# A two-block fp32 layer stack on one Trainium2 core: five of the second block's first twelve projection chunks as split products, their low parts made by adding transfers

## The chip, the cores and the metric

The kernel runs on one core of one Trainium2 chip. The metric is the device time of one execution in microseconds. The kernel before was timed three times: median 1872.24 us, lowest 1869.12, highest 1878.97.

## What is computed

The input x is 256 tokens by 1024 features, fp32. Two blocks follow each other, each with two layers. The first block has in each layer a mixer of three branches (a state space branch, a latent attention, a gated recurrence), a cross attention to 256 memory rows and a feed-forward part of width 2816. The second block, where the change is, does in each layer:

```python
h = rmsnorm_2(x, g_attn[l])
proj = jnp.einsum('bsd,dc->bsc', h, w_in[l])          # 1024 -> 2304
qa, ka, va, qb, kb, vb = jnp.split(proj, offs, axis=-1)
...
x = x + jnp.einsum('bsm,md->bsd', y, w_out[l])
h = rmsnorm_2(x, g_ffn[l])
gate, val = jnp.split(jnp.einsum('bsd,df->bsf', h, w_up[l]), 2, axis=-1)
gate = centred_dwconv(gate, conv_w[l], conv_b[l])
x = x + jnp.einsum('bsf,fd->bsd', jax.nn.silu(gate) * val, w_down[l])
```

## The kernel before, in words

All activations stay on the chip; the weights stream through once. A weight chunk is 128 partitions by up to 1024 fp32 values (512 KB). SyncE loads the chunks in the order in which TensorE's program names them into a ring of four slots (W, RSLOTS, line 1254); chunk n may be loaded when chunk n-4 is released (chunk_release).

There are two ways to multiply. **Whole**: TensorE takes the fp32 chunk from W as it is (product, line 400; the trace has two rows for one such matmul). **Split, in halves**: every operand is a high part, rounded to fp32r, and a low part, the rest; three products, high x high, high x low and low x high, go to the same bank (line 402). A split chunk has a high part in WH and a low part in WL, each a ring of three slots (HSLOTS). The list splits says who makes the low part: "dve" and "pool" mean that ScalarE copies W to WH (split_to of ScalarE, line 1465) and DVE or POOL then subtracts (low_parts, line 1178); "both" means that POOL does both (both_parts, lines 1349 and 1351). The release of a whole chunk is TensorE's last matmul on it, that of a split chunk the making of its low part. In the first block's gate projections every other chunk of 256 rows by 512 columns is "both" and the ones between are whole; their input has its halves made by POOL (halves_of, lines 1368 and 1369) in mix_half, which lies in the tile HTL.

**Around the change.** Each feed-forward part ends with four banks of 128 tokens by 512 columns, finished in the order of bank_order (last_two). DVE adds each bank to X (add_bank, line 2117). TensorE transposes X into banks "hT" 0 to 3, two groups of 128 features each (raw_T, line 492): hT 0 and 1 ahead of the last bank's products, hT 2 and 3 after the first chunk of the next projection, since they need the last sums. ScalarE evicts hT 0 and 2 (whole_cols of ScalarE, the copies of line 1465 into M), DVE hT 1 and 3 (whole_cols of DVE, lines 2104 and 2105); the input of the projections, HT2, lies in M. Between these ScalarE takes the sums of squares (sum_of, line 1505), from which POOL makes the root of the norm (norm_rstd, lines 1306 to 1317). The root is applied at the eviction of the projections, so TensorE doesn't wait for it.

In the first layer of the second block there is the first block's final norm too: DVE scales X (line 2636), ScalarE takes its squares again (line 1929), and POOL makes the mask of the attention window (lines 1428 to 1431), which ScalarE copies to fp32r.

The second block's projections are p2 0 to p2 4 (proj, token_steps): p2 0 to 3 of 512 columns in four chunks of 256 input rows (k0 = 0, 2, 4, 6), p2 4 of 256 columns in two chunks. All are whole. p2 0, 1 and 2 are TensorE's first work of the layer, with the transposes of the first results (qk_T) between them; p2 3 and 4 are spread between the attention's heads. ScalarE evicts each bank twice, squares (line 1945) and values (take_proj, line 1566); DVE then norms and rotates the heads (norm_rope, lines 2663 to 2694), and TensorE transposes these.

## Time and profile before

| | |
|---|---|
| three runs, median | 1872.24 us (1869.12 to 1878.97) |
| profiled execution, its own time | 1873.33 us |
| its span in the trace | 1871.5 us |
| mean granted TensorE clock | 0.99 |
| TensorE matmuls busy | 95% |
| VectorE (DVE) busy | 66% |
| ScalarE (ACT) busy | 47% |
| GpSimd (POOL) busy | 14% |
| bytes read from HBM | 271.78 MB |

The page lists busy time by engine, the chain of work that ended last, and groups of instructions by line and tile. Times in the trace are microseconds from the span's start. PE is TensorE's matmuls, PEld its weight loads, SPq and POOLq the queues that issue DMAs. A row such as "W,M" names what is read: for a matmul the moving operand first, the stationary one second. "issue" is time in which the engine waited for nothing that the profile shows. A clock of 1.00 is 2.4 GHz, 0.50 is 1.2 GHz.

### The profile page before, as it was taken

How to read it: one execution, taken by the hardware profiler on the slowest of the kernel's cores; microseconds unless marked ns; L12 is line 12 of the kernel's file. 1: busy time of each engine (PE TensorE's matmuls, PEld its weight loads, DVE VectorE, ACT ScalarE, POOL GpSimd, SP SyncE). 2: the span in 40 equal slices, each digit the busy share in tenths (PEclk: the TensorE clock that was granted, in tenths of full speed). 3: DMA queues.
4: the chain of work that ended last, by engine and by line, in shares of the span. 5: the costliest groups of instructions: out<-in, count | busy, mean ns of one | idle time of the engine just before them, and what ended most of it. 6: DMA issues, size and time to landing. Idle time of an engine off the chain costs nothing.

```text
span 1871.5 us, 27092 instructions
## 1 busy us (share of the span) xinstructions
PE 1786.2 (95%) x10038; PEld 1437.7 (77%) x10038; DVE 1236.3 (66%) x1903; ACT 872.1 (47%) x1421; POOL 255.6 (14%) x262
## 2 busy tenths in 40 slices
PE   7999999989999999999989999998999999899998
PEld 6676667679998856668578998656899874679987
DVE  7996746555667893756556566565677746566775
ACT  4224455464344422445455445446555543555553
POOL 4015553010000002455111000100100000010000
PEclk9999999999999999999999999999999999999999
DMA  6445442445556444444254666431455644235664
GB/s 162 135 131 157 135 158 91 156 127 171 160 183 190 114 131 130 158 135 158 78 170 144 186 184 192 142 119 57 135 173 181 196 149 124 68 113 171 181 189 136
DMA packets 192359, 274.61 MB, mean 147 GB/s; under 512 B 25616, under 2 KB 129540, under 8 KB 192228
## 3 DMA queue, kind: packets, MB, share of 16 engines
q1 hardware_dynamic: 191364, 269.86, 47.1%
q0 software_dynamic: 864, 3.02, 0.5%
q8 instruction: 80, 1.31, 0.3%
q14 instruction: 51, 0.42, 0.1%
HBM read 271.78 MB, written 1.05 MB: 146 GB/s over the span
## 4 chain that ended last, share of the span: by engine, by line
PE 86%; DVE 6%; ACT 3%; issue 2%; SPq 1%; DMA 0%; POOL 0%; DVEq 0%; ACTq 0%; POOLq 0%
PE bank L402 52%; PE bank L400 24%; DVE WL L1178 2%; PE bank L676 2%; PE bank L590 1%; PE bank L1034 1%; ACT WH L1465 1%; PE bank L598 1%; PE bank L877 1%; PE bank L492 1%; PE bank L1054 1%; ACT HTH L1465 1%; DVE HTL L2179 1%; PE bank L647 0%; PE bank L659 0%
## 5 line engine op out<-in xcount | busy, mean ns | idle before, releaser
L1178 DVE TENSOR_TENSOR WL<-W,WH 128x1024 fp32r<-128x1024 f32 x312 | 382.3, 1225 | 251.5 <-ACT WH L1465 243.1
L1465 ACT ACTIVATE WH<-W 128x1024 fp32r<-128x1024 f32 x332 | 351.8, 1060 | 273.9 <-PE bank L402 241.3
L402 PE MATMUL bank<-HTH,WH 128*128 128x256 f32 x1536 | 439.7, 286 | 13.2 <-issue 5.2
L402 PE MATMUL bank<-HTL,WH 128*128 128x256 f32 x1536 | 435.9, 284 | 0.0
L402 PE MATMUL bank<-HTH,WL 128*128 128x256 f32 x1536 | 435.9, 284 | 0.0
L402 PEld LDWEIGHTS bank<-HTH,WH 128*128 128x128 f32 x1536 | 296.0, 193 | 18.1 <-issue 11.6
L402 PEld LDWEIGHTS bank<-HTL,WH 128*128 128x128 f32 x1536 | 296.0, 193 | 0.2
L402 PEld LDWEIGHTS bank<-HTH,WL 128*128 128x128 f32 x1536 | 296.0, 193 | 0.0
L402 PE MATMUL bank<-WH,HTL 128*128 128x512 f32 x672 | 262.0, 407 | 0.0
L402 PE MATMUL bank<-WH,HTH 128*128 128x512 f32 x480 | 193.6, 403 | 17.6 <-ACT M L1594 11.4
L402 PE MATMUL bank<-WL,HTH 128*128 128x512 f32 x480 | 188.9, 394 | 0.0
L400 PE MATMUL bank<-W,M 128*128 128x512 f32 (+1 forms) x416 | 166.2, 555 | 2.6 <-issue 2.6
L402 PEld LDWEIGHTS bank<-WH,HTL 128*128 128x128 f32 x672 | 127.3, 189 | 32.3 <-issue 5.3
L400 PE MATMUL bank<-W,HTF 128*128 128x512 f32 (+1 forms) x384 | 149.8, 539 | 0.0
L400 PEld LDWEIGHTS bank<-W,M 128*128 128x128 f32 x416 | 79.2, 194 | 75.7 <-issue 72.9
L402 PEld LDWEIGHTS bank<-WH,HTH 128*128 128x128 f32 x480 | 91.1, 190 | 42.0 <-issue 16.3
L400 PEld LDWEIGHTS bank<-W,HTF 128*128 128x128 f32 x384 | 68.2, 190 | 67.5 <-issue 66.1
L1306 POOL TENSOR_SCALAR QSQ<-QSQ 128x2 f32<-128x2 f32 x9 | 5.5, 608 | 762.3 <-ACT PB L1505 762.3
L402 PEld LDWEIGHTS bank<-WL,HTH 128*128 128x128 f32 x480 | 91.3, 190 | 18.2
L400 PE MATMUL bank<-HTF,W 128*128 128x256 f32 x448 | 99.6, 381 | 0.6 <-DVE HTF L2428 0.6
L400 PEld LDWEIGHTS bank<-HTF,W 128*128 128x128 f32 x448 | 84.3, 190 | 13.2 <-issue 1.1
L1351 POOL TENSOR_TENSOR WL<-W,WH 128x1024 fp32r<-128x1024 f32 x36 | 88.9, 2469 | 2.9
(405 smaller groups left out, 2445.6 us busy)
## 6 DMA issues: line engine op xcount, KB each, us to landing
W<-in_w_in SPq DMA_DIRECT2D x132, 512.0 KB, 3.7
W<-in_ffn_w_gate_up SPq DMA_DIRECT2D x176, 256.0 KB, 3.3
W<-in_w_up SPq DMA_DIRECT2D x176, 256.0 KB, 3.5
W<-in_ffn_w_down SPq DMA_DIRECT2D x44, 512.0 KB, 4.3
W<-in_w_down SPq DMA_DIRECT2D x44, 512.0 KB, 4.3
W<-in_w_out SPq DMA_DIRECT2D x32, 512.0 KB, 3.3
W<-in_ssm_w_glu SPq DMA_DIRECT2D x16, 512.0 KB, 4.3
W<-in_x_w_kv SPq DMA_DIRECT2D x16, 512.0 KB, 3.9
```

The lines of the kernel that those rows point to most:

```text
L400: return pe.matmul(out, at_a(a), at_b(b), start=start, stop=stop, skip_group_check=True)
L402: m = pe.matmul(out, at_a(a[x]), at_b(b[y]), start=(start and i == 0), stop=(stop and i == 2), skip_group_check=True)
L492: m = pe.transpose(ps[:, k * S + tt * P:k * S + tt * P + P], X[:, tt, (2 * j + k) * P:(2 * j + k) * P + P], IDENT[:, :])
L590: ins = pe.matmul(ps[:, tt * S:tt * S + S], qT[:, tt * P:tt * P + P], kT, start=(tt == 0), stop=(tt == TT - 1), skip_group_check=True)
L598: ins = pe.transpose(ps[:, kt * S + tt * P:kt * S + tt * P + P], p_buf(tag, m[1])[:, tt, kt * P:kt * P + P], IDENT[:, :])
L676: m = pe.matmul(ps[:, h * P:h * P + P], ka[:, h, b * P:b * P + P], qa[:, h, b * P:b * P + P], start=(h == 0), stop=(h == HGH - 1), skip_gr ...
L877: m = pe.matmul(ps[64 * (h % 2):64 * (h % 2) + 64, 0:S], vtok[:, kt, h * VD:h * VD + VD], PT[h % 2][:, kt, :], start=(kt == 0), stop=(kt = ...
L1034: pe.matmul(ps[:, tt * S:tt * S + S], qkT[r:r + 64, h // 2, tt * P:tt * P + P], qkT[r:r + 64, 4 + h // 4, :], start=(tt == 0), stop=False, ...
L1054: m = pe.matmul(ps[:, h * HD:h * HD + HD], t_buf("a2", h)[:, kt, tt * P:tt * P + P], proj2[:, kt, 640 + (h // 4) * HD:640 + (h // 4) * HD ...
L1178: eng.tensor_tensor(WL[:, m % HSLOTS, 0:width], W[:, n % RSLOTS, 0:width], h, ALU.subtract)\
L1351: signal(pool.tensor_tensor(low, raw, high.bitcast(F32), ALU.subtract), s, v)
L1465: copy = lambda dst, src, scale=1.0: act.activation(dst, src, ACT.Copy, scale=scale)
```

## The change

Of the twelve chunks of p2 0, 1 and 2 in each layer of the second block, five become split: k0 = 6 of p2 0, k0 = 2 and 6 of p2 1 and of p2 2. The split kind is new, "dma": ScalarE writes the negative of the rounded chunk into WL, then the high part into WH, and POOL issues a DMA that adds the chunk from HBM once more onto WL (add_chunk, accum_op), which leaves the low part. The slot in W is released when ScalarE has made the high part. The two chunks of a pair are named, and so loaded, the split one first; TensorE uses them in the old order (in_pairs).

The split input is made by POOL from HT2 with halves_of into mix_half: first k = 2, 3, then k = 6, 7. TensorE waits for both (in2_halves) after the transposes that follow p2 0's first chunk. In the second block's first layer POOL's root of the final norm goes behind this work, and the mask of the window, which stood behind the root, goes ahead of it. ScalarE makes the first chunk's copies after its third sum of squares and ahead of the eviction of hT 2, the second chunk's after the fourth sum, the third's ahead of the evictions of p2 0, the last two chunks' ahead of those of p2 1.

```diff
--- before.py
+++ after.py
@@ -319,14 +319,24 @@
-            who = "dve" if splits[m][1] == "dve" else "pool"
-            return f"low_{who}", sum(1 for _, w in splits[:m + 1] if (w == "dve") == (who == "dve"))
+            who = splits[m][1]
+            if who == "dma":
+                return f"low_dma{m % HSLOTS}", 16 * sum(1 for _, w in splits[m % HSLOTS:m + 1:HSLOTS] if w == "dma")
+            if who == "dve":
+                return "low_dve", sum(1 for _, w in splits[:m + 1] if w == "dve")
+            return "low_pool", sum(1 for _, w in splits[:m + 1] if w in ("pool", "both"))
...
+        def negative_done(m):
+            return sum(1 for _, w in splits[:m + 1] if w == "dma")
@@ -358,21 +368,45 @@
-            def chunk(name, srcs, k, cols, low="dve"):
+            def declare(name, srcs, k, cols, low="dve"):
...
                 chunks.append((name, srcs, k, cols))
-                if low is None:
+                if low is not None:
+                    m = split_of[n] = len(splits)
+                    splits.append((n, low))
+                    chunk_release[n] = ("high", high_done(m)) if low == "dma" else low_done(m)
+                return n
+            def operands(n):
+                _, _, k, cols = chunks[n]
+                shaped = lambda t, i: t[:, i, 0:k * cols].rearrange("p (k n) -> p k n", k=k)
+                if n not in split_of:
                     pe.wait_ge(sem[f"w_full{n % RSLOTS}"], raw_full(n))
-                    return n, W[:, n % RSLOTS, 0:k * cols].rearrange("p (k n) -> p k n", k=k)
-                m = len(splits)
-                splits.append((n, low))
-                split_of[n] = m
+                    return shaped(W, n % RSLOTS)
+                m = split_of[n]
+                if splits[m][1] == "dma":
+                    pe.wait_ge(sem["high"], high_done(m))
                 s, v = low_done(m)
                 pe.wait_ge(sem[s], v)
-                chunk_release[n] = (s, v)
-                return n, [w[:, m % HSLOTS, 0:k * cols].rearrange("p (k n) -> p k n", k=k) for w in (WH, WL)]
+                return [shaped(w, m % HSLOTS) for w in (WH, WL)]
+            def chunk(*args):
+                n = declare(*args)
+                return n, operands(n)
+            def in_pairs(tag, wname, l, K, c0, cols, kstep, added):
+                n = {}
+                for k0 in range(0, K, 2 * kstep):
+                    for k in (k0 + kstep, k0) if k0 + kstep in added else (k0, k0 + kstep):
+                        n[k] = declare(tag, rows(wname, l, k, kstep, c0, cols), kstep, cols, "dma" if k in added else None)
+                    yield n[k0]
+                    yield n[k0 + kstep]
@@ -407,12 +441,19 @@
-            def token_steps(tag, wname, l, act, K, c0, cols, low="dve", kstep=2, halves=None):
+            def token_steps(tag, wname, l, act, K, c0, cols, low="dve", kstep=2, halves=None, added=()):
                 ps = [begin(*tag, tt) for tt in range(TT)]
+                if added:
+                    numbers = in_pairs(tag, wname, l, K, c0, cols, kstep, added)
                 for k0 in range(0, K, kstep):
                     src, slot = act, lambda k: k
-                    if halves and k0 // kstep % 2:
+                    if added:
+                        n = next(numbers)
+                        if k0 in added:
+                            src, slot = halves, half_slot
+                        w = operands(n)
+                    elif halves and k0 // kstep % 2:
                         n, w = chunk(tag, rows(wname, l, k0, kstep, c0, cols), kstep, cols, "both")
@@ -1024,7 +1065,8 @@
                     return token_steps(("p2", l, j), "w_in_2", l, HT2, KT, 512 * j, 512 if j < 4 else 256, low=None,
-                                       kstep=kstep)
+                                       kstep=kstep, halves=mix_half if j < 3 else None,
+                                       added=(() if j > 2 else (2, 6) if j else (6,)))
@@ -1095,6 +1137,7 @@
                             raw_T(nrm - 1, i, ("f2d", l - 1) if l else ("ffd", DEPTH - 1))
+                        pe.wait_ge(sem["in2_halves"], 2 * l + 2)
                     for _ in steps:
@@ -1350,11 +1393,23 @@
+            def add_chunk(m):
+                n, _ = splits[m]
+                _, (src,), k, cols = chunks[n]
+                pool.wait_ge(sem["negative"], negative_done(m))
+                dst = WL[:, m % HSLOTS, 0:k * cols].rearrange("p (k n) -> p k n", k=k)
+                pool.dma_start(dst, src, accum_op=ALU.add).then_inc(sem[low_done(m)[0]], 16)
...
                         both_parts(m)
+                        lows[0] = m + 1
+                    elif splits[m][1] == "dma":
+                        add_chunk(m)
                         lows[0] = m + 1
@@ -1422,17 +1477,29 @@
                 .then_inc(sem["final_gain"], 16)
-            norm_rstd(nrm)
-            nrm += 1
...
+                first = split_before["p2", l, 0, TT - 1] - 1
+                wait_full(pool, (*(("f2d", l - 1) if l else ("ffd", DEPTH - 1)), *bank_order[-1]))
+                wait_freed(pool, ("hT", nrm + (l == 0), 1))
+                signal(halves_of(mix_half, HT2, 2), "in2_halves", 2 * l + 1)
+                split_to(first + 1)
+                wait_freed(pool, ("hT", nrm + (l == 0), 3))
+                signal(halves_of(mix_half, HT2, 6), "in2_halves", 2 * l + 2)
+                if l == 0:
+                    norm_rstd(nrm)
+                    nrm += 1
+                split_to(first + 2)
                 norm_rstd(nrm, halves=l > 0)
                 nrm += 1
+                split_to(first + 5)
                 for g in range(DFH):
@@ -1483,6 +1550,8 @@
                         act.wait_ge(sem[s], v)
+                    if who == "dma":
+                        signal(copy(WL[:, m % HSLOTS, 0:width], W[:, n % RSLOTS, 0:width], -1.0), "negative", negative_done(m))
                     signal(copy(WH[:, m % HSLOTS, 0:width], W[:, n % RSLOTS, 0:width]), "high", high_done(m))
@@ -1906,8 +1975,10 @@
             sum_of(nrm, ("ffd", DEPTH - 1), 0, 1, 2)
+            split_to(split_before["p2", 0, 0, TT - 1])
             whole_cols(nrm + 1, HT2, final_gain, 2)
             sum_of(nrm, ("ffd", DEPTH - 1), 3)
+            split_to(split_before["p2", 0, 0, TT - 1] + 1)
             nrm += 1
@@ -1920,8 +1991,10 @@
                     sum_of(nrm, ("f2d", l - 1), 0, 1, 2)
+                    split_to(split_before["p2", l, 0, TT - 1])
                     whole_cols(nrm, HT2, own_gain, 2)
                     sum_of(nrm, ("f2d", l - 1), 3)
+                    split_to(split_before["p2", l, 0, TT - 1] + 1)
                 else:
@@ -1934,6 +2007,9 @@
+                    if j < 2:
+                        split_to(split_before["p2", l, 0, TT - 1] + 2 * j + 2)
                     for tt in range(TT):
```

## Rows read from the trace of the kernel before

**Rows 1.** The page: busy time by engine; shares of the chain that ended last.
```profile
PE 1786.2 (95%) x10038; PEld 1437.7 (77%) x10038; DVE 1236.3 (66%) x1903; ACT 872.1 (47%) x1421; POOL 255.6 (14%) x262
...
PE 86%; DVE 6%; ACT 3%; issue 2%; SPq 1%; DMA 0%; POOL 0%; DVEq 0%; ACTq 0%; POOLq 0%
```

**Rows 2.** The chain in the gate stage, layer 1: start us, us, what.
```profile
747.90 2.73 PE bank L402 x12
750.64 3.43 PE bank L400 x8
```

**Rows 3.** TensorE's timeline, second block: start us, us, engine, line, operation, tiles, count.
```profile
1195.87 1.04 PE L492 MATMUL bank<-IDENT,X 128*128 128x128 f32 x8
1196.74 24.20 PE L400 MATMUL bank<-W,M 128*128 128x512 f32 x56
...
1221.65 13.90 PE L400 MATMUL bank<-W,M 128*128 128x512 f32 x32
1235.39 0.60 PE L1022 MATMUL bank<-IDENT,M 128*128 128x128 f32 x4
...
1532.83 24.20 PE L400 MATMUL bank<-W,M 128*128 128x512 f32 x56
```

**Rows 4.** The timeline of ScalarE, DVE and POOL beside it, both layers.
```profile
1193.66 0.19 ACT L1505 ACTIVATION_READ_ACCUMULATOR PB<-X 128x1 f32 x1
1196.51 0.98 ACT L1465 ACTIVATE M<-bank,PAR 128x256 f32<-128x256 f32 x2 [2.66 <-PE bank L492]
...
1198.06 0.19 ACT L1505 ACTIVATION_READ_ACCUMULATOR PB<-X 128x1 f32 x1
...
1197.54 0.48 DVE L2105 TENSOR_SCALAR M<-bank,PAR 128x256 f32<-128x256 f32 x1
...
1198.39 0.19 POOL L1309 TENSOR_TENSOR SSQ<-QSQ 128x2 f32<-128x2 f32 x1 [4.85 <-ACT PB L1505]
...
1533.63 0.48 DVE L2105 TENSOR_SCALAR M<-bank,PAR 128x256 f32<-128x256 f32 x1
1534.15 2.25 DVE L2653 TENSOR_TENSOR TB<-RC,BT 128x64 f32<-128x64 f32 x16
```

**Rows 5.** POOL's instructions on the tile HTL: durations in ns, forms.
```profile
L1368 POOL CAST HTL<-HTF x4: 609/610/758, 135.9 to 728.8; 128x512 fp32r<-128x512 f32 x4
L1369 POOL TENSOR_TENSOR HTL<-HTF,HTL x4: 1263/1268/2126, 136.7 to 729.5; 128x512 fp32r<-128x512 f32 x4
```

**Rows 6.** The page's costliest groups: ScalarE's copies of a chunk.
```profile
L1465 ACT ACTIVATE WH<-W 128x1024 fp32r<-128x1024 f32 x332 | 351.8, 1060 | 273.9 <-PE bank L402 241.3
```

**Rows 7.** The timeline of ScalarE and DVE later in the projections, layer 0.
```profile
1208.02 0.69 ACT L1945 ACTIVATE TB<-bank,RSTD 128x512 f32<-128x512 f32 x1 [2.06 <-issue]
...
1219.32 0.69 ACT L1945 ACTIVATE TB<-bank,RSTD 128x512 f32<-128x512 f32 x1 [8.46 <-PE bank L400]
...
1232.32 0.42 DVE L2688 TENSOR_TENSOR A<-A,TB 128x256 f32<-128x256 f32 x1
```

**Rows 8.** DMA issues: KB each, median us from issue to landing.
```profile
W<-in_w_in SPq DMA_DIRECT2D x132, 512.0 KB, 3.7
...
M<-in_norm_final POOLq DMA_DIRECT2D x1, 512.0 KB, 7.5
```

**Rows 9.** Stretches (busy us by engine, granted clock, DMA) and TensorE's timeline there.
```profile
488.00:490.00 2.00, 0.00 (x0) 0.01 (x1) 1.83 (x6) 0.00 (x0) 0.00 (x0) 1.00 0.76 221
490.00:493.40 3.40, 3.37 (x16) 3.40 (x17) 2.09 (x5) 1.85 (x4) 0.00 (x0) 0.50 0.17 60
1295.60:1302.40 6.80, 5.57 (x14) 4.44 (x15) 3.90 (x8) 4.16 (x13) 0.00 (x0) 0.50 0.03 7
1358.00:1366.00 8.00, 6.31 (x53) 6.14 (x52) 6.09 (x10) 4.37 (x7) 0.00 (x0) 1.00 0.52 171
...
1296.84 0.77 PE L402 MATMUL bank<-WH,HTH 128*128 128x512 f32 x1 [5.72 <-ACT M L1594]
...
1361.68 0.35 PE L402 MATMUL bank<-HTH,WH 128*128 128x256 f32 x1 [1.69 <-issue]
```

## The prediction

> **What bounds the kernel now.** The page comes first: TensorE is busy for 95% of the span and is 86% of the chain that ended last [rows 1]. So a microsecond taken from TensorE's products is a microsecond of the kernel, unless the products then wait. Next come the chain in the gate stage, which already alternates whole and halved chunks of this very size, and TensorE's timeline around the changed stage. A chunk of 256 input rows by 512 columns costs 3.43 us whole (eight rows of L400) and 2.73 us in halves (twelve rows of L402) [rows 2]. In the second block's layer 0 the projections run without a gap: a first chunk, the transposes of the input's second half at 1195.87, then seven chunks from 1196.74, two transposes, four chunks from 1221.65, end at 1235.39 [rows 3]. Layer 1 has the same pattern at 1532.83. Here nothing but TensorE is late.
>
> **What the change takes away.** Five chunks of twelve per layer go from 3.43 to 2.73 us: 5 x 0.70 = 3.5 us per layer, **7.0 us in both**, 0.37% of the time. A measurement of this kernel can tell about 0.5%, 9.4 us, from no change; so the full gain would not be seen.
>
> **The new wait on TensorE.** The split input (mix_half) has to be made by POOL, and TensorE waits for all of it (in2_halves at 2l+2) straight after the transposes, ahead of the second chunk, though only the fourth chunk of that projection uses it. Behind this wait stand the second, whole chunk and all else on TensorE. Its cost in layer 0: DVE ends the eviction of k = 6, 7 at 1197.54 + 0.48 = 1198.02; POOL starts some 0.14 us after another engine's signal (its sum at 1198.39 after ACT's read that ends at 1198.25) [rows 4]; POOL makes a half in a cast of 0.61 and a subtraction of 1.27 us, with 0.1 us between, 2.0 us [rows 5]. So the halves are there at 1200.1, TensorE goes on at about 1200.3 in place of 1196.74, and **3.5 us** are lost. The other half (k = 2, 3) is hidden: its input is out before the first chunk starts, and POOL has the length of that chunk and of the transposes for it. In layer 1 the eviction ends at 1534.11, 0.1 us later against its transposes, and DVE then runs sixteen small products with two SBUF inputs, 2.25 us long, beside POOL's subtraction [rows 4]. Rows 5 show that subtraction at 1.26 to 2.13 us. I take 0.4 us more for layer 1; bounds 0 and 0.9. The two stalls make **7.4 us**.
> The Trainium skill (SBUF — State Buffer, Who interferes with whom) says that a DVE instruction with two SBUF inputs holds off a GpSimd instruction that reads SBUF; by that, layer 1 would be at the upper bound. The longest subtraction of rows 5 fits it, but the trace does not show that it is the cause.
>
> **The clock.** After 5.72 us without a matmul the rows show TensorE at half its rate: the granted clock is 0.50 of 2.4 GHz, that is 1.2 GHz, for 6.8 us, of which 1.2 still fell into the idle time. After 2.0 us it was 0.50 for 3.4 us. After 1.69 us it stayed at 1.00 [rows 9]. An idle time of 3.5 us lies between the two that cost. 3.4 us at half speed lose 1.7 us, 6.8 us less 1.2 lose 2.8 us. I take 1.7 per layer, the row that 3.5 is nearest to: **3.4 us**, bounds 0 and 5.6.
>
> **What ScalarE gets.** Ten copies of 1.06 us per layer (minus the weights, then their high part) [rows 6], 10.6 us. Cover in layer 0: the first two start after the third sum, at 1193.9, and end by 1196.0, before the eviction that starts at 1196.51 [rows 4]. The second two wait for a load into the slot that TensorE frees at 1195.87; with the 3.7 us of rows 8 they run from 1199.6 to 1201.8. Evictions began at 1208.02 [rows 7]; the third pair goes ahead of them, so they begin at 1210.2, where the first projection now ends at 1209.9. The last four lie in the 8.46 us in which ScalarE waited for the second projection [rows 7]; they end at about 1219.5 (the last load follows a chunk that TensorE ends at 1213.3), that projection's first bank at 1220.8. If this cover were gone, each pair would put 2.1 us on the evictions. DVE's norm and rotation of the second projection ended at 1232.74, 2.65 us before TensorE wanted them at 1235.39 [rows 3, 7]; it starts about 1.3 us later, so 1.4 us stay. Cost: nothing; bounds 0 and 2 us per layer.
>
> **POOL and the queues.** In layer 0 POOL's root for the final norm goes behind the halves, 2 us later. It feeds the evictions through DVE and ScalarE; even 1.9 us later these would meet the first projection's new end. In layer 1 the root waits for a load and a copy, until about 1539.5, while the first projection ends at about 1546. On SP the loads keep their count, but an added chunk stands ahead of its partner and its slot is free once ScalarE has copied it. The whole chunk behind it is issued when TensorE ends the second chunk, 1203.7, lands at 1207.4 and is wanted at 1209.9: hidden by 2.5 us. The band mask is made earlier. Nothing.
>
> **The adding transfers.** No row shows one. From the end of the negative copy (POOL free) to TensorE's use, layer 0 gives: 1195.0 to 1207.2, 1201.4 to 1213.3, 1209.1 to 1219.5, 1214.1 to 1226.5, 1218.4 to 1232.7; the shortest is **10.4 us**. The nearest rows: 512 KB from SP's queue land in 3.7 us, 512 KB from POOL's in 7.5 us [rows 8]. The lower bound is 3.7; for the upper I double 7.5, since an add has more to do than a load: 15. I take 7.5, the same queue and size: cost 0.
> The Trainium skill (DMA: Bandwidth & Descriptors, Anatomy of one DMA — SWDGE (gpsimd) path) gives a plain transfer on this path 2.0 us plus its bytes by 436 GB/s; an estimate from that page is 3.2 us for 512 KB, and the cost is 0 by it too. The row measured more than twice that.
>
> **The sum.** -7.0 + 7.4 + 3.4 = **+3.8 us**. The profiled execution was 1873.33 us, 1871.5 its span; it goes to 1877.1. The median of the three runs, 1872.24, is 1.1 us below it, so I predict **1876.0 us**.
>
> **The rivals.**
> A, the adds are late: slower. An add stands between ScalarE's copy and the chunk; it decides from 10.4 us on. At 15 us the first is late by 2.8, the second by 0.3, the third by 1.8, the fourth by 0.5 (each lateness lengthens the next one's time): 5.4 per layer, 11 in both, 1887 with the rest. For: accumulating is untried here, and four of five budgets are under 12.5. Against: 7.5 us in the row. Chance 0.13.
> B, the wait without the clock: an idle time of 3.5 us leaves it at 1.00. Then 1872.6. Against: 2.0 us was enough once. For: 1.69 was not. Chance 0.16.
> C, POOL at its slowest, 0.9 us more in each layer, and the clock down for 6.8 us both times: +1.4 and +2.2 on the forecast, 1880; with a copy pair exposed, 1882. Chance 0.12.
> D, TensorE does not stall: the wait is met early and the 7.0 us stay, 1865 to 1869. It would need POOL to be done by 1196.74, before DVE has even evicted its input. Chance 0.04.
> That halving does nothing at all is excluded by rows 2, if these chunks run like the gates'.
> The forecast itself: 0.55.
>
> **How the numbers follow.** Slower by over 0.5% (above 1881.6): nearly all of A, 0.12, half of C, 0.06, and 0.04 of the forecast's case by the unknown copies: 0.22. Faster by over 0.5% (below 1862.9): no case reaches it; 0.02 for what I overlook. Within: 0.76. The range goes from 1868, the upper part of D, to 1886, most of A. B and the forecast lie within it.
>
> **What would show it.** After the transposes of the first projection TensorE idles some 3.5 us, released by POOL's subtraction into HTL, in both layers. The granted clock is 0.50 for 3.4 us or more behind it. Halved chunks show as 2.73 us at full clock, and the projections of layer 0 then end some 2 us later than at 1235.39 against the end of the block before. POOL's add lands within 10 us and no L402 matmul waits on WL. ScalarE's evictions of the second projection start when its bank is full. It is wrong if TensorE waits for a DMA, if no idle time stands behind the transposes, or if the clock stays at 1.00.

## The result, and the profile after

The kernel after took **1886.37 us** (median of six runs, 1883.77 to 1893.46); the kernel before, timed beside it, 1874.46 us (six runs, 1869.12 to 1885.58). The ratio is **1.0066, 95% interval 1.0041 to 1.0090**: the medians are 11.9 us apart and the ratio makes it 12.4 us slower, where 3.8 were forecast. 1886.37 lies 0.4 us above the range of the prediction, and "the same within 0.5%" was given 0.76. Of the 10.4 us between it and the forecast of 1876.0, 2.2 are the kernel before itself, whose median was 1872.24 us when the forecast was made. The profiled execution took 1884.42 us, its span 1882.5, 11.0 more than before.

The page first, the rows that answer to [rows 1]: TensorE's busy time fell by 4.7 us while the span grew by 11.0, so the time is in waits. The chain has more DVE (6 to 8%) and 1% of DMA.

```profile
PE 1781.5 (95%) x10078; PEld 1444.7 (77%) x10078; DVE 1240.3 (66%) x1903; ACT 893.1 (47%) x1441; POOL 274.3 (15%) x280
...
PE 83%; DVE 8%; ACT 4%; issue 2%; DMA 1%; POOL 0%; SPq 0%; DVEq 0%; ACTq 0%; POOLq 0%
```

Next TensorE's timeline in the second block, the answer to [rows 3]; brackets hold the idle time before a row and who ended it. (L434, L436, L533 and L1063 of this kernel are L400, L402, L492 and L1022 of the one before.) Layer 0:

```profile
1193.23 3.59 PE L434 MATMUL bank<-W,M 128*128 128x512 f32 x8
1196.66 1.04 PE L533 MATMUL bank<-IDENT,X 128*128 128x128 f32 x8
1200.88 8.82 PE L434 MATMUL bank<-W,M 128*128 128x512 f32 x16 [3.18 <-POOL HTL L1424]
...
1222.63 0.47 PE L436 MATMUL bank<-WH,HTL 128*128 128x512 f32 x1 [0.55 <-DMA WL<-in_w_in]
...
1228.13 1.95 PE L1063 MATMUL bank<-IDENT,A 128*128 128x128 f32 x8 [2.52 <-DVE A L2764]
1229.88 4.46 PE L434 MATMUL bank<-W,M 128*128 128x512 f32 x8
...
1245.68 1.10 PE L1076 MATMUL bank<-TB 64*128 64x256 f32 x4 [1.54 <-issue]
```

and layer 1:

```profile
1536.29 3.59 PE L434 MATMUL bank<-W,M 128*128 128x512 f32 x8
...
1543.99 7.13 PE L434 MATMUL bank<-W,M 128*128 128x512 f32 x16 [3.24 <-POOL HTL L1424]
...
1554.69 3.67 PE L434 MATMUL bank<-W,M 128*128 128x512 f32 x8 [0.81 <-DMA W<-in_w_in]
...
1566.47 0.47 PE L436 MATMUL bank<-WH,HTL 128*128 128x512 f32 x1 [1.90 <-DMA WL<-in_w_in]
1570.69 1.09 PE L1063 MATMUL bank<-IDENT,A 128*128 128x128 f32 x8 [1.24 <-DVE A L2764]
```

I measure everything from here on by the **stage**: from the first matmul of the projections to the first 64x256 matmul of the scores (the row at 1245.68). Before it took 45.44 us in layer 0 (1192.44 to 1237.88) and 45.45 in layer 1; after, 52.45 and 50.28. That is +7.0 and +4.8, together **+11.8**. The rest nearly cancels: 0.8 us later at the stage's start, and in layer 1 the low clock that the profile before has just behind the stage (1575.4 to 1578.9, 1.7 us lost) is missing after.

The granted clock (column 0.50 or 1.00) in the stretches behind the two long waits of layer 0, and behind the wait of layer 1:

```profile
1200.90:1204.30 3.40, 3.40 (x4) 1.49 (x5) 1.96 (x2) 1.56 (x2) 1.14 (x3) 0.50 0.71 130
1228.20:1231.60 3.40, 3.40 (x11) 2.37 (x12) 2.94 (x11) 1.89 (x4) 0.00 (x0) 0.50 0.86 162
...
1544.00:1547.40 3.40, 3.40 (x8) 1.62 (x9) 1.65 (x13) 2.11 (x2) 1.39 (x2) 1.00 0.67 122
```

Layer 0 fell to 1.2 GHz twice; no row of layer 1's stage is below 1.00.

Why DVE was late stands in the timelines of ScalarE, DVE and POOL, the answer to [rows 4, 7]:

```profile
1202.70 1.06 ACT L1532 ACTIVATE WL<-W 128x1024 fp32r<-128x1024 f32 x1 [3.61 <-issue]
...
1213.41 1.06 ACT L1532 ACTIVATE WL<-W 128x1024 fp32r<-128x1024 f32 x1 [5.47 <-DMA W<-in_w_in]
...
1215.59 0.69 ACT L2021 ACTIVATE TB<-bank,RSTD 128x512 f32<-128x512 f32 x1
...
1217.83 1.22 DVE L2739 TENSOR_REDUCE HSSQ<-TB 128x16 f32<-128x1024 f32 x1 [8.95 <-ACT TB L2021]
...
1227.39 0.69 DVE L2764 TENSOR_TENSOR A<-A,TB 128x512 f32<-128x512 f32 x1
...
1199.57 1.26 POOL L1424 TENSOR_TENSOR HTL<-M,HTL 128x512 fp32r<-128x512 f32 x1
...
1215.02 1.26 POOL L1403 DMA_DIRECT2D WL<-in_w_in  x1 [4.98 <-ACT WL L1532]
```

The copies of the third chunk start at 1213.41, because ScalarE waits 5.47 us for the chunk's load, and the evictions stand behind them: 1215.59 in place of 1208.02. DVE's chain, reduce to rotation, takes 10.3 us, and ends at 1228.08; TensorE, at 1225.61 done with the second projection, waits for it 2.52 us. These are the results of the first projection; for them DVE had hardly anything to spare in the kernel before, ready at 1220.22 for 1220.78:

```profile
1219.53 0.69 DVE L2688 TENSOR_TENSOR A<-A,TB 128x512 f32<-128x512 f32 x1
...
1220.78 1.04 PE L1022 MATMUL bank<-IDENT,A 128*128 128x128 f32 x8
```

The load that the third pair waits for, in SyncE's queue and in the view of the DMA issues of 1206.7 to 1208: it is issued 0.41 us behind the whole chunk's, which went out at 1206.29 when TensorE had ended its second chunk, and lands after 6.5 us.

```profile
1206.70 0.79 SPq L1297 DMA_DIRECT2D W<-in_w_in  x1
...
W<-in_w_in SPq DMA_DIRECT2D x1, 512.0 KB, 6.5
```

The DMA issues in 1190 to 1245, after (KB each, median us to landing),

```profile
W<-in_w_in SPq DMA_DIRECT2D x12, 512.0 KB, 5.7
WL<-in_w_in POOLq DMA_DIRECT2D x5, 512.0 KB, 6.6
```

and before:

```profile
W<-in_w_in SPq DMA_DIRECT2D x13, 512.0 KB, 3.6
```

The loads slowed from 3.6 to 5.7 us (5.0 in the repetition of the kernel after, experiment 10). Over both layers the ten adds landed in 5.8 to 8.8 us, median 7.2; 7.5 was taken.

### The profile page after: what moved, and what is told of

It reads as the page before. It is cut to its first block, busy times and chain, and to the rows that moved or that the text cites. A ratio compares the mean times of both kernels' runs of the same rounds, so it can differ in the third digit from the quotient of the medians.

```text
span 1882.5 us, 27236 instructions
## 1 busy us (share of the span) xinstructions
PE 1781.5 (95%) x10078; PEld 1444.7 (77%) x10078; DVE 1240.3 (66%) x1903; ACT 893.1 (47%) x1441; POOL 274.3 (15%) x280
## 4 chain that ended last, share of the span: by engine, by line
PE 83%; DVE 8%; ACT 4%; issue 2%; DMA 1%; POOL 0%; SPq 0%; DVEq 0%; ACTq 0%; POOLq 0%
PE bank L436 52%; PE bank L434 21%; DVE WL L1221 2%; PE bank L717 2%; PE bank L631 1%; ACT WH L1532 1%; PE bank L1076 1%; PE bank L533 1%; PE bank L639 1%; DMA W<-in_w_in 1%; PE bank L918 1%; PE bank L1096 1%; ACT HTH L1532 1%; DVE HTL L2255 1%; PE bank L688 0%
## 5 line engine op out<-in xcount | busy, mean ns | idle before, releaser
L1532 ACT ACTIVATE WH<-W 128x1024 fp32r<-128x1024 f32 x342 | 362.4, 1060 | 273.3 <-PE bank L436 240.3
L436 PE MATMUL bank<-HTH,WH 128*128 128x256 f32 x1536 | 439.1, 286 | 13.2 <-issue 5.2
L436 PE MATMUL bank<-HTL,WH 128*128 128x256 f32 x1536 | 435.2, 283 | 0.0
L436 PE MATMUL bank<-HTH,WL 128*128 128x256 f32 x1536 | 435.2, 283 | 0.0
L436 PEld LDWEIGHTS bank<-HTH,WH 128*128 128x128 f32 x1536 | 295.2, 192 | 18.0 <-issue 11.6
L436 PEld LDWEIGHTS bank<-HTL,WH 128*128 128x128 f32 x1536 | 295.4, 192 | 0.2
L436 PEld LDWEIGHTS bank<-HTH,WL 128*128 128x128 f32 x1536 | 295.2, 192 | 0.0
L436 PE MATMUL bank<-WH,HTL 128*128 128x512 f32 x752 | 291.8, 410 | 2.4 <-DMA WL<-in_w_in 2.4
L436 PE MATMUL bank<-WH,HTH 128*128 128x512 f32 x480 | 193.6, 403 | 17.3 <-ACT M L1663 11.5
L436 PE MATMUL bank<-WL,HTH 128*128 128x512 f32 x480 | 188.9, 394 | 0.0
L436 PEld LDWEIGHTS bank<-WH,HTL 128*128 128x128 f32 x752 | 142.4, 189 | 41.1 <-issue 11.5
L434 PE MATMUL bank<-W,HTF 128*128 128x512 f32 (+1 forms) x384 | 149.8, 539 | 0.0
L434 PE MATMUL bank<-W,M 128*128 128x512 f32 (+1 forms) x336 | 135.7, 555 | 9.8 <-POOL HTL L1424 6.4
L436 PEld LDWEIGHTS bank<-WH,HTH 128*128 128x128 f32 x480 | 91.2, 190 | 41.6 <-issue 15.9
L434 PEld LDWEIGHTS bank<-W,HTF 128*128 128x128 f32 x384 | 68.2, 190 | 67.5 <-issue 66.1
L434 PEld LDWEIGHTS bank<-W,M 128*128 128x128 f32 x336 | 65.5, 200 | 63.2 <-issue 52.6
L436 PEld LDWEIGHTS bank<-WL,HTH 128*128 128x128 f32 x480 | 91.4, 190 | 18.1
L434 PE MATMUL bank<-HTF,W 128*128 128x256 f32 x448 | 99.6, 381 | 0.6 <-DVE HTF L2504 0.6
L434 PEld LDWEIGHTS bank<-HTF,W 128*128 128x128 f32 x448 | 84.5, 191 | 13.1 <-issue 1.1
L1635 ACT ACT_TABLE_LOAD x16 | 20.5, 1283 | 93.9 <-PE bank L436 49.6
```

Of the source, the lines that this page charges most:

```text
L434: return pe.matmul(out, at_a(a), at_b(b), start=start, stop=stop, skip_group_check=True)
L436: m = pe.matmul(out, at_a(a[x]), at_b(b[y]), start=(start and i == 0), stop=(stop and i == 2), skip_group_check=True)
L1532: copy = lambda dst, src, scale=1.0: act.activation(dst, src, ACT.Copy, scale=scale)
L1635: free_after(act.activation(dst, bank(name)[:, 0:width], func, scale=scale), *name)
```

## The experiments

All variants are of the kernel after. Each batch has its own runs of the kernel before, whose median varied from 1873.9 to 1880.3 us between batches; so the ratio of one batch carries some 0.3% that is not the variant's, and the stages are the finer measure. They are from the profiled executions, in us. Two cautions go with them. The kernel after itself gave +11.8 in one profile and +7.9 in another, so differences of under 4 us between single profiles of the variants that keep its early wait decide nothing. And the stage ends at a matmul, while a low clock often stands right behind it: from that matmul to the second one of its kind it is 4.88 us at full clock, and what a profile shows above that, in both layers together, is the column "clock behind".

| kernel | stage 0 | stage 1 | both, against before | clock behind | ratio to before, 95% |
| --- | --- | --- | --- | --- | --- |
| before | 45.44 | 45.45 | | 1.7 | |
| after | 52.45 | 50.28 | +11.8 | 0.0 | 1.0066 (1.0041 to 1.0090) |
| after, again | 49.60 | 49.15 | +7.9 | 1.7 | 1.0049 (1.0029 to 1.0070) |
| wait alone | 50.66 | 48.97 | +8.7 | 1.7 | 1.0033 (1.0019 to 1.0047) |
| wait late | 45.66 | 46.48 | +1.3 | 0.0 | 1.0002 (0.9979 to 1.0025) |
| small adds | 48.87 | 47.14 | +5.1 | 0.0 | one run, 1876.83 us |
| copies behind | 49.67 | 51.26 | +10.0 | 1.7 | 1.0059 (1.0038 to 1.0079) |
| third chunk early | 46.70 | 43.44 | -0.8 | 1.7 | 1.0001 (0.9982 to 1.0020) |
| four chunks | 45.36 | 46.24 | +0.7 | 5.0 | 1.0054 (1.0035 to 1.0073) |
| early, small adds | 43.24 | 42.06 | -5.6 | 1.7 | one run, 1869.78 us |
| low parts by DVE | 45.17 | 42.06 | -3.7 | 1.7 | 0.9983 (0.9966 to 0.9999) |
| and transposes later | 44.32 | 42.06 | -4.5 | 5.0 | 0.9963 (0.9946 to 0.9980) |
| the same, again | 44.33 | 42.06 | -4.5 | 3.3 | 0.9983 (0.9967 to 1.0000) |
| before, again | 45.45 | 45.44 | 0.0 | 0.0 | 0.9990 (0.9966 to 1.0014) |

**1. The wait alone.** All twelve chunks whole again, no copies, no adds; POOL still makes the split input and TensorE still waits for it.

```diff
-   kstep=kstep, halves=mix_half if j < 3 else None, added=...)
+   kstep=kstep)
-   split_to(split_before["p2", l, 0, TT - 1])
...
```

Every new split_to, ScalarE's and POOL's, goes in the same way.

> All twelve chunks stay whole, with no copies by ScalarE and no adding transfers; only POOL's making of the split input and TensorE's wait for it stay from the change. Stage here means the time from the first matmul of the projections to the first attention score: 45.4 us in both layers before, 52.5 and 50.3 after the change. My theory: the wait leaves TensorE idle for 3.2 to 3.4 us in each layer, and the clock falls behind it for 3.4 us in one layer or both (1.7 us each), so each stage is 49 to 51 us long and the kernel 7 to 10 us slower than before. Rival (the idle time is taken up later by slack, as DVE's norm and rotation were ahead of TensorE): stages within 1 us of 45.4, the kernel the same as before.

TensorE's rows in layer 0 and 1, and the clock behind the waits:

```profile
1203.00 26.00 PE L434 MATMUL bank<-W,M 128*128 128x512 f32 x56 [3.26 <-POOL HTL L1423]
...
1544.14 24.30 PE L434 MATMUL bank<-W,M 128*128 128x512 f32 x56 [3.25 <-POOL HTL L1423]
```

```profile
1204.30:1207.70 3.40, 3.40 (x5) 1.35 (x4) 3.13 (x5) 1.78 (x3) 0.04 (x1) 0.50 0.01 2
1545.00:1548.40 3.40, 3.40 (x9) 1.52 (x8) 0.80 (x6) 0.00 (x0) 0.56 (x1) 1.00 0.02 5
```

The same seven chunks take 26.00 us in layer 0 and 24.30 in layer 1: the clock's price is 1.7 us, and it is paid in one layer. The stages are 5.2 and 3.5 longer. This is near the predicted +7.4 and +3.4 without its second clock term, and as expected. The wait alone makes the stages 8.7 us longer and the kernel 0.33% slower (6.2 us; the interval reaches to 8.8).

**2. The wait late.** TensorE waits for the split input ahead of the fourth chunk, which uses it.

```diff
+   next(steps)
+   next(steps)
    pe.wait_ge(sem["in2_halves"], 2 * l + 2)
```

> The changed kernel, with TensorE's wait for the split input moved from ahead of the second chunk to ahead of the fourth, the first that uses it. My theory: no idle time behind the transposes and no fall of the clock there, 3.3 and 5.0 us less; the load that ScalarE's third pair of copies waits for is issued 3 to 5 us earlier. In layer 0 the root of the norm, ready at 1210, now bounds the evictions, so TensorE waits some 3 us for DVE ahead of the first results' transposes; stages of 47 to 49 us (layer 0) and 44 to 47 us (layer 1), the kernel 6 to 9 us faster than the changed one. Rival (ScalarE's copies bound the stage whatever TensorE does): the idle time moves as a whole to the wait for DVE, stages stay over 50 us.

What is left of waits, layer 0 and then layer 1:

```profile
1212.65 0.47 PE L436 MATMUL bank<-WH,HTL 128*128 128x512 f32 x1 [2.04 <-DMA WL<-in_w_in]
1222.88 1.09 PE L1063 MATMUL bank<-IDENT,A 128*128 128x128 f32 x8 [0.98 <-DVE A L2766]
...
1563.14 1.61 PE L1063 MATMUL bank<-IDENT,A 128*128 128x128 f32 x8 [1.89 <-DVE A L2766]
```

Moving one line takes 10.5 of the 11.8 us away, or 6.6 of the 7.9 of the repeated kernel after; the wait alone cost 8.7. It does not bring the 7 us of the halves: without the stall TensorE is early, and now it is an add (the second chunk's, 2.04 us) and DVE that are late. Layer 0 lost less than expected (47 to 49 us were). The ratio of 1.0002 agrees: the change with its worst wait taken out is worth nothing.

**3. Small adds.** The adds move 64 of the 512 columns of each 128 rows, so the rest of the low part is not made. Everything else is the kernel after.

```diff
-   pool.dma_start(dst, src, accum_op=ALU.add)
+   pool.dma_start(dst[:, :, 0:64], src[:, :, 0:64], accum_op=ALU.add)
```

> The changed kernel, with each adding transfer cut to the first 64 of its 512 columns (64 KB in place of 512 KB); the rest of the low part is not made right. Theory of contention: the adds share the DMA engines with SyncE's loads; without them the loads land in 4 to 5 us in place of 5.7 (median), ScalarE's third pair starts 1 to 3 us earlier, no chunk waits for its add, and both stages get 2 to 4 us shorter. Rival (the third pair waits because its load stands in SyncE's queue behind one that TensorE releases): its start moves by under 1 us, the wait for DVE stays at 1 to 2.5 us, and only the 0.5 and 1.9 us of the late adds go.

The same window's DMA issues, and the wait for DVE in layer 0:

```profile
W<-in_w_in SPq DMA_DIRECT2D x12, 512.0 KB, 3.9
WL<-in_w_in POOLq DMA_DIRECT2D x5, 64.0 KB, 3.4
```

```profile
1225.44 1.09 PE L1063 MATMUL bank<-IDENT,A 128*128 128x128 f32 x8 [1.53 <-DVE A L2764]
```

The loads are back at 3.9 us: it was the adds' traffic that slowed them. The waits for a DMA are gone, but most of the wait for DVE stays: 1.53 us in layer 0, for 2.52 and 2.19 in the two profiles of the kernel after, and 1.34 in layer 1, for 1.24 and 1.51. In layer 0 the evictions start 20.5 us into the stage (1212.91, the stage begins at 1192.45), for 22.4 and 21.2 in the kernel after. So the traffic makes them 0.8 to 1.9 us late and is not the main cause. The expectation's rival is the nearer one: the third split chunk is loaded behind a whole chunk that waits for TensorE.

**4. Copies behind.** ScalarE makes the third pair of copies behind the first projection's evictions.

```diff
-   if j < 2:
-       split_to(split_before["p2", l, 0, TT - 1] + 2 * j + 2)
+   if j == 1:
+       split_to(split_before["p2", l, 0, TT - 1] + 4)
...
+   if j == 0:
+       split_to(split_before["p2", l, 0, TT - 1] + 2)
```

The last two lines stand behind the evictions.

> The changed kernel, with ScalarE's third pair of copies moved behind the evictions of the first projection. My theory: the evictions start at about 1211 in layer 0 (1215.6 after the change), DVE is done before TensorE wants it, and the 2.5 and 1.2 us of wait for DVE and the clock's fall behind it go; in exchange the third chunk's add is issued 2 to 3 us later and TensorE waits for it by 1 us more. Stages of 48 to 50 us in both layers, the kernel 3 to 5 us faster than the changed one. Rival (the evictions were not what held DVE, or the late add costs as much): stages as in the changed kernel, 52 and 50 us.

ScalarE's eviction, then TensorE's wait, in layer 0:

```profile
1214.25 0.69 ACT L2021 ACTIVATE TB<-bank,RSTD 128x512 f32<-128x512 f32 x1 [4.54 <-PE bank L436]
```

```profile
1227.34 0.47 PE L436 MATMUL bank<-WH,HTL 128*128 128x512 f32 x1 [2.23 <-ACT WH L1532]
```

The evictions start 18.0 us into the stage, 4.4 earlier than in the kernel after (3.2 than in its repetition), and no matmul waits for DVE. In its place the third add, issued at 1218.73, is late: TensorE waits 2.23 us for it, 2.13 in layer 1. (The row names ScalarE, whose next copy ended at that moment; the matmul reads the pair copied at 1217.13, and layer 1's row names the DMA.) So it is shown that the pair ahead of the evictions is what makes DVE late, and that behind them it has no room either. The gain of 3 to 5 us that was expected did not come: stage 0 is as long as in the repeated kernel after (49.67 and 49.60). Of stage 1's 51.26 us, 1.7 are a low clock behind the wait for POOL, which this profile has in layer 1 too, and some 1.4 another one behind the late add (0.60 on average from 1573.0 to 1576.4):

```profile
1549.16 8.83 PE L434 MATMUL bank<-W,M 128*128 128x512 f32 x16 [3.24 <-POOL HTL L1424]
```

**5. Third chunk early.** With the wait late, the loads are named in the order 0, 6, 2, 4 for the first projection and 2, 6, 0, 4 for the others, so that no split chunk stands behind a whole one that frees its slot late; ScalarE copies the third pair before it waits for the norm's root.

```diff
-   for k in (k0 + kstep, k0) if k0 + kstep in added else (k0, k0 + kstep):
+   for k in (0, 6, 2, 4) if added == (6,) else (2, 6, 0, 4):
```

> The changed kernel with TensorE's wait late (as in the run that moved it) and the loads in another order: the first projection's split chunk second, the second and third projection's two split chunks ahead of their whole ones, so that the third pair's load goes into a slot that ScalarE has freed itself; ScalarE makes the third pair before it waits for the norm's root. Theory (the third pair stood behind a load that TensorE releases, and held the evictions): evictions start 16 to 17 us after the stage's first matmul in layer 0 and at 15 to 16 in layer 1, no wait for DVE, stages of 42.5 to 43.5 us, 2 to 3 us under the kernel before in each layer; the kernel 4 to 6 us faster than before. Rival (the adding transfers are late whatever the order, because they share the DMA engines with loads that now come in a bunch): TensorE waits 2 us or more for an add in each layer, stages of 45 us or more.

```profile
1213.35 0.47 PE L435 MATMUL bank<-WH,HTL 128*128 128x512 f32 x1 [2.71 <-DMA WL<-in_w_in]
...
1549.42 0.47 PE L435 MATMUL bank<-WH,HTL 128*128 128x512 f32 x1 [1.13 <-DMA WL<-in_w_in]
```

```profile
DMA to landing us min/median/max: 5.8/8.0/9.2
```

Evictions now start at 1210.05, 17.0 us into the stage, and no wait for DVE is left. Layer 1 gains 2.0 us. But the adds now land in up to 9.2 us (the last row is that of its WL tile in 1190 to 1245), and the second is 2.7 us late in layer 0, with a low clock of 3.4 us behind it. Beside experiment 2, which has the wait late too, the waits for DVE of 0.98 and 1.89 us are gone; the loads' order and the place of the third pair, ahead of the root, were changed together and not tried apart. The next cause is the adds. Layer 0 missed the 42.5 to 43.5 us that were expected, and the kernel is not faster than before.

**6. Four chunks.** With the wait late, the second projection's last chunk is whole again.

```diff
-   added=(() if j > 2 else (2, 6) if j else (6,))
+   added=((6,), (2,), (2, 6), (), ())[j]
```

> The changed kernel with the wait late and only four split chunks in each layer: the last chunk of the second projection, whose copies stood ahead of the evictions, stays whole. Theory: nothing holds the evictions but the root (layer 0) and the products; DVE waits no more for copies; TensorE waits some 2 us for DVE in layer 0, where the root bounds, and under 0.5 us in layer 1; stages 44.5 to 45.5 and 42.5 to 43.5 us. Rival (the adds' traffic is what makes the loads late, and four adds are nearly as many as five): TensorE still waits over 1 us for a load or an add in both layers, stages of 45.5 us and more.

```profile
1224.02 1.06 ACT L1534 ACTIVATE WL<-W 128x1024 fp32r<-128x1024 f32 x1 [6.68 <-DMA W<-in_w_in]
...
1235.70 0.69 ACT L2023 ACTIVATE TB<-bank,RSTD 128x512 f32<-128x512 f32 x1 [5.39 <-PE bank L436]
```

```profile
1239.40 0.66 PE L1063 MATMUL bank<-IDENT,M 128*128 128x128 f32 x4 [2.43 <-DVE A L2766]
```

One split chunk fewer did not help. A pair of copies now waits 6.68 us for its load, at the head of ScalarE's queue, the second projection's evictions come behind it, and the second transposes wait for DVE (2.43 us, 2.94 in layer 1). The expected gain did not come. The ratio of 1.0054 is more than the stages' +0.7 explains. Part of it stands right behind them: the new waits come directly ahead of the stage's end, and the clock falls behind them in both layers (column "clock behind": 5.0 us for 1.7 before). For the rest see the last section.

```profile
1579.40:1586.20 6.80, 6.80 (x12) 3.31 (x13) 4.11 (x15) 3.25 (x8) 0.00 (x0) 0.53 0.01 2
```

**7. Early, small adds.** Experiment 5 with the adds of experiment 3, which leave most of the low part unmade.

```diff
-   for k in (k0 + kstep, k0) if k0 + kstep in added else (k0, k0 + kstep):
+   for k in (0, 6, 2, 4) if added == (6,) else (2, 6, 0, 4):
...
-   pool.dma_start(dst, src, accum_op=ALU.add)
+   pool.dma_start(dst[:, :, 0:64], src[:, :, 0:64], accum_op=ALU.add)
```

> The early order with the wait late, each adding transfer cut to 64 of 512 columns; the rest of the low part is not made right. If the adds' traffic costs nothing in this order, the stages are within 0.5 us of those with whole adds; if they share the DMA engines with the loads to TensorE's cost, the stages are 1 us or more shorter. The least that is possible is about 42.2 us: 45.4 less 3.5, and 0.3 for the slower first matmul of each halved chunk.

Stages 43.24 and 42.06. Without the adds' cost layer 1 gains 3.4 us, which is the halves' full saving, and layer 0 gains 2.2 (a wait of 0.92 us for DVE is left). So the whole adds cost 4.8 us in this order. This is what the change could be worth: 5.6 us, 0.3%.

**8. Low parts by DVE.** Experiment 5, but DVE subtracts as in the rest of the kernel; no adds.

```diff
-   "dma" if k in added else None
+   "dve" if k in added else None
```

> The early order of loads with the wait late, and the low parts made by DVE's subtraction in place of the adding transfer: no second read of the chunks, one copy on ScalarE in place of two, 1.23 us on DVE for each of five chunks. Theory (the traffic of the adds and their 7 us cost more than DVE's time is worth): loads land in 4 us, no wait for a DMA; two subtractions fall between the first two norm-and-rotate runs and use up the 2.6 us that DVE was ahead of TensorE; stages of 42.5 to 44 us, the kernel 3 to 6 us faster than before and not slower than the run with the adds in the same order. Rival (DVE bounds the stage): TensorE waits over 2 us for DVE ahead of the transposes, stages of 45 us or more.

```profile
1220.35 1.09 PE L1062 MATMUL bank<-IDENT,A 128*128 128x128 f32 x8 [2.09 <-DVE A L2765]
```

DVE has room for the five subtractions in layer 1 (42.06, no wait for DVE) and not in layer 0, where 2.09 us come back before the first transposes: the expectation held in one layer and its rival in the other.

**9. Transposes later.** Experiment 8, with the first results' transposes behind the second chunk of the third projection.

```diff
    pe.wait_ge(sem["in2_halves"], 2 * l + 2)
+   if j == 2: next(steps); next(steps); qk_T(0, (0, 1))
```

> The run with the low parts by DVE, and the transposes of the first projection's results moved from ahead of the third projection into it, behind its second chunk. Theory: TensorE's 2.1 us of wait for DVE in layer 0 are covered by the two chunks that now come first (6.2 us); stages of 42 to 43 us in both layers, 2.4 to 3.4 us under the kernel before; the kernel 5 to 7 us faster than before. Rival (DVE is the bound and the wait comes back at the second projection's transposes): layer 0 stays at 44.5 to 45.2 us.

```profile
1233.34 0.66 PE L1062 MATMUL bank<-IDENT,M 128*128 128x128 f32 x4 [2.12 <-DVE A L2767]
```

The wait moved to the second transposes nearly whole, 2.12 us: in layer 0 DVE's own work is the bound, as the rival had it. The stage is 0.85 us shorter than in experiment 8, but the wait now stands directly ahead of the stage's end, and behind it the clock falls for 6.8 us:

```profile
1234.90 1.67 PE L1075 MATMUL bank<-TB 64*128 64x256 f32 x4 [0.47 <-issue]
...
1243.12 1.13 PE L1075 MATMUL bank<-TB 64*128 64x256 f32 x4
```

The two rows are 8.22 us apart for 4.88 at full clock: 3.3 us go back, more than the stage gained. The ratio is the best of the versions that keep the whole computation, 0.9963, but no run separates it from experiment 8.

**10. The kernel after, again,** in that batch.

> The changed kernel once more, beside the run before on the same chip. Theory: 0.4 to 0.9% slower than the kernel before, with idle times behind the transposes (3.2 us) and ahead of the first results' transposes (1 to 3 us) in both layers. Rival (the first measurement was a matter of the chip): ratio within 0.2% of 1.

Ratio 1.0049 (1.0029 to 1.0070). Its profile has 3.18 us for POOL and 2.19 for DVE in layer 0, and 3.24, 1.59 for an add and 1.51 for DVE in layer 1; this time no clock fell behind the wait for DVE. The slowdown repeats; whether it is above 0.5% is left open by both intervals.

**11. The kernel before, again, and the version of experiment 9, again.**

> The kernel before, unchanged, against itself. If the comparison is sound its ratio lies within 0.2% of 1 (0.998 to 1.002); if the batch alone can make 0.4%, the best version's gain means nothing. Its profile is the second one of the kernel before. Theory C1: the long stretches of granted clock 0.50 in the second block's attention (17 to 27 us in six of the variants' profiles, none over 6.8 us in the profile of before) come with the chip and the execution, so that this profile has one as well and its attention stages are 102 to 105 us in at least one layer. Theory C2: they come with the variants' different timing, so that the attention stages are 97 to 99 us again, with no low stretch over 7 us.

> The last version once more (wait late, third load early, low parts by DVE, first transposes after the second chunk of the third projection). Its projection stages are 44.3 and 42.1 us again, within 0.3 us. Under C2 (the variant's own timing brings the long low stretch) its profile shows a stretch of 17 us or more at 0.50 in the same layer, near 1280 to 1297 us. Under C1 (chance of the execution) it may be absent or in the other layer. Ratio under either 0.994 to 0.998; if the first result was luck of the batch, 0.999 or more.

The stages of the second repeat to 0.01 us, the ratio is 0.9983 (0.9967 to 1.0000), the same as experiment 8's, and no long stretch of low clock is in its profile. The kernel before against itself gives 0.9990 (0.9966 to 1.0014), but its second profile is 12.6 us longer than the first, with the same stages (45.45 and 45.44). Its granted clock in layer 0's attention (column 0.50 or 1.00):

```profile
1270.00:1284.00 14.00, 13.60 (x83) 11.37 (x81) 5.71 (x13) 8.14 (x23) 0.00 (x0) 1.00 0.23 76
1284.00:1301.10 17.10, 17.10 (x63) 13.55 (x63) 6.96 (x14) 8.61 (x20) 0.00 (x0) 0.50 0.00 0
```

A second such stretch stands at 1625.3 to 1642.4. So the variants' timing is not needed for them (C2 falls): the unchanged program has them in one execution and not in another.

The two ratios of the version of experiment 9 are 0.37 and 0.17% below 1; the stages' 4.5 us are 0.24%, of which the clock behind them takes 1.6 to 3.3 us back. So it beats the kernel after for certain and the kernel before by 0.2% at best, which is hardly more than the kernel before against itself shows.

## Why the prediction was wrong, step by step

- **What bounds the kernel**: right. All that was lost was lost as waits of TensorE in the changed stage.
- **The halves, -7.0 us**: nearly right. A whole and a halved chunk together take 6.20 us (1212.29 to 1218.49) for 6.86 before: -6.6 in all. Experiments 7 and 8 show the full 3.4 us in a layer without waits.
- **The new wait, 7.4 us**: right. TensorE resumed 7.65 us after the stage's start in layer 0 and 7.70 in layer 1, for 4.30 before: 3.35 + 3.40 = 6.75. The idle times of 3.18 and 3.24 do not show all: each wait costs some 0.17 more, since one group's tail no longer overlaps the next one's start.
- **The clock, 3.4 us**: its size was right, its places half. 1.7 was paid behind the wait in layer 0 in all five kernels that have the early wait (both profiles of the kernel after, experiments 1, 3 and 4), and in layer 1 only in experiment 4. The other 1.7 of this profile stands behind the wait for DVE.
- **The adding transfers, 7.5 us and a cost of 0**: the size was right (7.2), the cost not. Waits of 0.55, 0.81 and 1.90 us for an add or a load are 3.3 us. The shortest budget, 10.4 us, counted from the copies' end as I had placed them; the third copies came later, and with them the third add: issued at 1215.02, landed at 1222.6. And I had not asked what the adds do to the loads: 3.6 to 5.7 us.
- **"What ScalarE gets ... Cost: nothing; bounds 0 and 2 us per layer"**: this is **the step that failed**. The third pair was put at 1208.0, by a load of 3.7 us from 1203.7 on. In SyncE's queue that load stands behind that of a whole chunk, which goes out only when TensorE has released a slot, after the stall and the slow clock; and it lands later still beside the adds. The pair started at 1213.41, 5.4 us later: 0.8 is the stage's own later start, 1.7 the slow clock, which the forecast had in its sum and not in this schedule, and 2.8 the landing, 6.5 us for 3.7. The evictions began 7.6 us later than before in place of 2.2, and DVE made TensorE wait for 2.52 and 1.24 us, 3.8 in all. The text set this lateness against the 2.65 us by which DVE was ahead with the second results; the first results, where the wait came, had 0.56 us to spare and were not looked at. Experiment 4 showed the pair's place as the cause, 3 the share of the adds' traffic, and 5 that an early load, with the pair ahead of the root, frees DVE.
- **The queues, "Nothing"**: wrong for the same reason. The release at 1203.7 had the stall in it but not the slow clock behind it, and the landing of every load was taken at 3.7 us, as if the adds were not there.

The sum as it should have been: -6.6 (halves) + 6.75 (POOL) + 3.4 (clock) + 3.3 (DMAs) + 3.8 (DVE) + some 0.85 for the five other waits' lost overlap = 11.5, against 11.8 measured. The forecast's miss of 8 us in the stages is DVE and the DMAs. The 0.17 us of a wait was read off the two waits for POOL and only carried over to the others. Of the rivals A had the right sign and too large an add; it is true in part, through the third add. (Its own sum: with an add of 15 us and each lateness carried over whole, the third is late by 1.5 and the fourth by nothing, 4.6 us per layer and not 5.4.) B, C and D fell: the idle time stayed near 3.2 us, POOL was never at its slowest, and TensorE did stall.

Of its own signs of being wrong one came true: TensorE waited for a DMA, three times.

Of the two rules weighed: the loads and adds of 512 KB took 5.7 and 6.6 us in this stage. By the Trainium skill (DMA: Bandwidth & Descriptors, Anatomy of one DMA — SWDGE (gpsimd) path) 3.2 was an estimate; experiment 3 measured 3.4 for an add of an eighth of the size, so the measurement decides, for adds too. The other rule is in the last section.

## What to carry to other kernels

Put a new wait directly ahead of the first instruction that needs what it waits for: here one line stood two chunks too early and cost more than the whole change could bring. When a copy is placed ahead of evictions, work out the landing of its load through the whole chain of slot releases, with the stalls that the change itself adds, because all that stands behind it on that engine inherits the lateness. And price a transfer's effect on its neighbours as well as its own latency.

## What the runs showed of the hardware that was not expected

**The clock in the attention.** The granted clock can be at 0.50 for 17.1 us while TensorE is busy all the time (17.10 of 17.10 us), right after 14 us at 1.00 with 13.60 busy, and with the DMA queues silent. The program before had two such stretches in one profile and none in the other, 12.6 us apart in span; 7.9 of these lie behind the first and the second stage, where the stretches are, and 4.7 ahead of the first stage. Of the variants' profiles those of experiments 2, 4, 5, 6, 8 and 9 had one; those of 1, 3, 7, 10, of the kernel after and of the repeated version of experiment 9 had none; in experiment 8 it lasted over 27 us. What starts them was not tried. The times show the same: the 105 executions of the kernel before in the later batches whose mean granted clock is 0.98 or more fall in two groups, 64 with 0.988 or more at 1868.2 to 1877.1 us and 41 with 0.987 or less at 1878.2 to 1885.9 us. How many of each a batch holds moves its ratio: experiment 1's ten executions have 0.987 to 0.989 and a median of 1883.5 us, and before's nine with 0.988 or more in that batch 1873.5, which is 9.9 us less, near the stages' 8.7, where the ratio says 6.2. This grouping was made with the results at hand, so it is a hint only. The stretches account for most of why the profiles of experiments 8 and 9, with 3.7 and 4.5 us less in the stages, had spans of 1871.0 and 1873.0 us for 1871.5 before, and probably for a part of experiment 6's ratio. They do not explain the loss that was studied: neither the profile of before nor that of after shown here has one.

**A similar wait, another clock.** 3.2 us of idle time were followed by 3.4 us at 0.50 in layer 0 in five profiles of five (the kernel after, its repetition, experiments 1, 3 and 4), and in layer 1 in one of the same five (experiment 4). No rule for that was found. After the 2.09 us of experiment 8 it stayed at 1.00, after the 2.12 us of experiment 9 it was 0.52 on average for 6.8 us.

**POOL beside DVE.** In layer 1 DVE's sixteen small products run beside POOL's halves. Before they took 2.25 us [rows 4]; after, DVE and POOL show

```profile
1541.90 3.74 DVE L2729 TENSOR_TENSOR TB<-RC,BT 128x64 f32<-128x64 f32 x16
```

```profile
1542.74 1.28 DVE L2729 TENSOR_TENSOR TB<-RC,BT 128x64 f32<-128x64 f32 x1
```

```profile
1542.68 1.26 POOL L1424 TENSOR_TENSOR HTL<-M,HTL 128x512 fp32r<-128x512 f32 x1
```

The prediction had POOL held off. It was DVE that lost 1.5 us: of its sixteen products one, begun at 1542.74, 0.06 us behind POOL's subtraction, lasted 1.28 us, about as long as the subtraction, which kept its 1.26 us. In experiment 8 POOL's cast, begun at 1532.22, 0.10 us behind DVE's subtraction of a chunk (1.23 us long), took 1.60 us for 0.61: there POOL was the one that lost. The Trainium skill (SBUF — State Buffer, Who interferes with whom) also says that the order of issue decides which of the two blocks; the trace agrees, and the prediction had used only half of the rule. TensorE did not wait for these products.

**An adding DMA on POOL's queue** holds POOL for 1.2 to 1.3 us to issue, and lands in 5.8 to 8.8 us for 512 KB in the kernel after, in up to 9.5 in experiment 4.
